# Expert output added to HBM as two scatters of 512 columns, empty places skipped, one gate product moved forward

## The reference, cut to what matters

```python
_, idx = lax.top_k(scores + router_bias, MOE_TOPK)          # 6 of 64 experts for each token
gate = gate / gate.sum(-1, keepdims=True) * ROUTED_SCALE
# routed_experts: token-slots sorted by expert, each expert's rows padded to whole blocks of 128
def run_block(args):
    tok, g, e = args
    return swiglu(x_pad[tok], w_exp_gu[e], w_exp_down[e]) * g[:, None]
return jnp.zeros((T + 1, D), xt.dtype).at[row_tok].add(out.reshape(R, D))[:T]
# moe: routed + swiglu(xt, w_sh_gu, w_sh_down); the layer: layer_norm(ALPHA * x + moe(x))
```

## Time and profile before

| | |
|---|---|
| runs, median (lowest to highest) | 2080.77 us (2078.91 to 2081.96) |
| profiled execution: its time, its span | 2079.63 us, 2077.8 us |
| busy share of PE, DVE, ACT, POOL | 94%, 45%, 27%, 30% |
| DMA in the loop over blocks | share 1.02 of 16 engines, 373 GB/s |
| granted TensorE clock in the loop | 1.00 (2.4 GHz) |

### The profile page before, as it was taken

How to read it: one execution, slowest core, us unless ns; L and a number is a source line. 1 busy time by engine, 2 the same in 40 slices (tenths; PEclk the granted TensorE clock), 3 DMA queues, 4 the chain that set the end, 5 groups by cost and what they waited for, 6 DMA issues and landing times.

```text
span 2077.8 us, 23451 instructions
## 1 busy us (share of the span) xinstructions
PE 1959.6 (94%) x7658; PEld 1084.7 (52%) x7658; DVE 929.9 (45%) x2467; ACT 562.7 (27%) x1147; POOL 618.8 (30%) x792
## 2 busy tenths in 40 slices
PE   8998999999999999999999899999999999999990
PEld 6786645666555665556555463444444444444440
DVE  4374465999765533030344743233332332332324
ACT  2223554562566640030233000111111111111114
POOL 0042000101220001101223254545445555555444
PEclk9999999999999999999999999999999999999995
DMA  6031212110110011134211406999999999999995
GB/s 189 3 38 14 64 41 102 41 47 5 26 26 3 1 31 48 44 132 126 103 61 48 155 31 217 376 369 373 381 373 375 378 373 376 375 373 377 375 364 193
DMA packets 130467, 365.09 MB, mean 176 GB/s; under 512 B 34641, under 2 KB 82514, under 8 KB 112594
## 3 DMA queue, kind: packets, MB, share of 16 engines
q1 hardware_dynamic: 105250, 289.80, 37.2%
q0 software_dynamic: 23328, 72.90, 13.6%
q10 hardware_dynamic: 1808, 1.33, 0.2%
HBM read 310.82 MB, written 53.04 MB: 175 GB/s over the span
## 4 chain that ended last, share of the span: by engine, by line
PE 55%; DMA 19%; DVE 8%; issue 7%; POOL 7%; ACT 2%; POOLq 0%; SPq 0%; DVEq 0%; ACTq 0%
DMA arena<-x_d,tid 17%; PE psum L630 11%; PE psum L774 9%; PE psum L792 6%; PE psum L645 4%; POOL arena L1293 3%; PE psum L845 3%; PE psum L444 3%; POOL acc_d L1287 2%; PE psum L479 2%; PE psum L708 2%; ACT arena L1341 2%; DVE arena L2264 2%; DMA acc_d<-arena,sid 2%; PE psum L491 2%
## 5 line engine op out<-in xcount | busy, mean ns | idle before, releaser
L1341 ACT ACTIVATE arena<-psum 128x512 f32<-128x512 f32 (+8 forms) x643 | 286.0, 486 | 1086.6 <-PE psum L918 429.7
L918 PE MATMUL psum<-arena 128*128 128x512 f32 x1088 | 484.3, 598 | 27.8 <-DVE arena L2264 24.9
L918 PEld LDWEIGHTS psum<-arena 128*128 128x128 f32 x1088 | 201.6, 190 | 267.2 <-issue 265.0
L1293 POOL DMA_INDIRECT arena<-x_d,tid x276 | 264.9, 960 | 85.8 <-issue 71.3
L932 PE MATMUL psum<-arena 128*128 128x512 f32 x544 | 244.7, 593 | 0.5 <-ACT arena L1341 0.5
L630 PE MATMUL psum<-arena 128*128 128x384 f32 (+1 forms) x768 | 239.7, 471 | 0.2 <-DMA arena<-in_w_glu 0.2
L2314 DVE TENSOR_TENSOR arena<-arena,psum 128x256 f32<-128x256 f32 x68 | 28.6, 421 | 457.7 <-ACT arena L1341 457.7
L630 PEld LDWEIGHTS psum<-arena 128*128 128x128 f32 x768 | 144.5, 190 | 94.7 <-issue 10.9
L774 PE MATMUL psum<-arena 128*128 128x384 f32 (+1 forms) x576 | 177.7, 472 | 1.1 <-DVE arena L2075 1.1
L2264 DVE STREAM_TRANSPOSE arena<-arena 128x256 f32<-128x256 f32 x272 | 150.3, 610 | 54.7 <-DMA arena<-x_d,tid 53.7
L932 PEld LDWEIGHTS psum<-arena 128*128 128x128 f32 x544 | 103.5, 190 | 130.0 <-issue 129.4
(11 more groups left out here) (313 smaller groups left out, 2148.1 us busy)
## 6 DMA issues: line engine op xcount, KB each, us to landing
arena<-in_w_exp_gu SPq DMA_DIRECT2D x69, 2048.0 KB, 10.4
arena<-in_w_exp_down SPq DMA_DIRECT2D x68, 1024.0 KB, 10.8
arena<-in_w_in SPq DMA_DIRECT2D x24, 512.0 KB, 4.5
arena<-in_x_prompt SPq DMA_DIRECT2D x10, 512.0 KB, 4.2
arena<-x_d,tid POOLq DMA_INDIRECT x276, 8.8
arena<-in_w_glu SPq DMA_DIRECT2D x16, 256.0 KB, 4.9
arena<-in_w_attn_proj SPq DMA_DIRECT2D x16, 256.0 KB, 4.5
arena<-in_w_out SPq DMA_DIRECT2D x1, 4096.0 KB, 14.4
```

Source lines behind the costliest of these rows:

```text
L918: last = mm(psum[:, 2, :], xgT[u][:, k, :], ewg[u][:, k, :], start=k == 0, stop=k == DK - 1)
L1293: pool.indirect_dma_start(xg[u][:, g, :], None, x1_d.rearrange("t (a f) -> (t a) f", a=4), bass.IndirectOffsetOnAxis(ap=tid[u][:, g:g + 1] ...
L1341: return act.activation(dst, src, fn, **kw)
```

## The change

Three things. Each scatter becomes two of 128 rows of 512 columns. `acc_d` is seen as 2T rows of 512, `sid` holds 2t and 2t + 1 for token t, and the semaphores `y_stored{u}` and `y_half` are split by half, so that a left half waits for the left half of the block before and a right half for the right. The indirect DMAs get a bound (`bounds_check`) of T tokens with `oob_is_err=False`, so that places whose number is T or more, the empty ones, are passed over. And `gate_shared(2)` is called ahead of the first `slots`, not behind the fifth. The rest is renaming: some semaphores are merged so that their number stays within the limit.

```diff
-            def scatter(u, rows_):
-                pool.indirect_dma_start(acc_d, bass.IndirectOffsetOnAxis(ap=sid[u][:, 0:1], axis=0), rows_, None,
-                                        compute_op=ALU.add).then_inc(s(f"y_stored{u}"), 16)
+            def scatter(u, j):
+                pool.indirect_dma_start(half_rows, bass.IndirectOffsetOnAxis(ap=sid[u][:, j:j + 1], axis=0),
+                                        yb[u][:, j * 512:(j + 1) * 512], None,
+                                        bounds_check=2 * T - 1, oob_is_err=False,
+                                        compute_op=ALU.add).then_inc(s(f"y_stored{u}{j}"), 16)
...
-                                            bass.IndirectOffsetOnAxis(ap=tid[u][:, g:g + 1], axis=0)
-                                            ).then_inc(s(f"xg_loaded{u}"), 16)
+                                            bass.IndirectOffsetOnAxis(ap=tid[u][:, g:g + 1], axis=0),
+                                            bounds_check=4 * T - 1, oob_is_err=False).then_inc(s(f"xg_loaded{u}"), 16)
...
-                    pool.wait_ge(s("carried"), n * 2 + 2)
-                    pool.wait_ge(s("sid_ready"), n + 1)
-                    pool.wait_ge(s("y_half"), n * 2 + 2)
-                    pool.wait_ge(s(f"y_stored{1 - u}"), ip * 16 + 16 + 16 * u)
-                    carry_wait()
-                    scatter(u, yb[u])
+                    for j in range(2):
+                        pool.wait_ge(s("carried"), n * 3 + 2 + j)
+                        pool.wait_ge(s("sid_ready"), n + 1)
+                        pool.wait_ge(s(f"y_half{j}"), n + 1)
+                        pool.wait_ge(s(f"y_stored{1 - u}{j}"), ip * 16 + 16 + 16 * u)
+                        carry_wait()
+                        scatter(u, j)
...
             gate_shared(1)
             dve.wait_ge(s("x1_stored"), 16 * NT)
+            gate_shared(2)
             for i in range(NT + 1):
-                if 2 <= i + 1 < NT and i > 0:
+                if 3 <= i + 1 < NT:
                     gate_shared(i + 1)
...
-                dve.wait_ge(s(f"y_stored{u}"), stores)
-                ts(sid[u][:], tab[:, 0, bass.ds(n, 1)], 1.0, None, ALU.mult).then_inc(s("sid_ready"), 1)
+                for j in range(2):
+                    dve.wait_ge(s(f"y_stored{u}{j}"), stores)
+                ts(sid[u][:, 0:1], tab[:, 0, bass.ds(n, 1)], 2.0, None, ALU.mult)
+                ts(sid[u][:, 1:2], tab[:, 0, bass.ds(n, 1)], 2.0, 1.0, ALU.mult, ALU.add).then_inc(s("sid_ready"), 1)
```

More of the change, by code:

```diff
@@ L280, in layer_program @@
         tab4, spread = at(46080, 4, NBP), at(46592, 4, 4, 32)
-        sid = [sb(f"sid{u}", [P, 1], I32) for u in range(2)]
+        sid = [sb(f"sid{u}", [P, 2], I32) for u in range(2)]
         dump = sb("dump", [P, 1])
@@ L1261, in _ @@
                 tt(x, x, ln1[0:r, 1, :], ALU.add).then_inc(s("x1_ready"), 1)
[L1264 to L1265 removed]
+            pool.wait_ge(s("states_and_zeros_stored"), 64 + 16 * 4)
+            pool.wait_ge(s("params_and_dump_ready"), 5)
+            half_rows = acc_d.rearrange("t (j f) -> (t j) f", j=2)
             for u in range(2):
[L1267 to L1270, removed]
+                for j in range(2):
+                    if u == 1:
+                        pool.wait_ge(s(f"y_stored0{j}"), 16)
+                    pool.indirect_dma_start(half_rows, bass.IndirectOffsetOnAxis(ap=sid[u][:, j:j + 1], axis=0),
+                                            ln1[:, u, j * 512:(j + 1) * 512], None, compute_op=ALU.add
+                                            ).then_inc(s(f"y_stored{u}{j}"), 16)
             pool.wait_ge(s("slots_ready"), 1)
@@ L1315, in _ @@
                     gather(1 - u)
-                    pool.wait_ge(s("carried"), n * 2 + 2)
-                    pool.wait_ge(s("sid_ready"), n + 1)
-                    pool.wait_ge(s("y_half"), n * 2 + 2)
-                    pool.wait_ge(s(f"y_stored{1 - u}"), ip * 16 + 16 + 16 * u)
-                    carry_wait()
-                    scatter(u, yb[u])
+                    for j in range(2):
+                        pool.wait_ge(s("carried"), n * 3 + 2 + j)
[4 more added lines that the diff above has]
+                        scatter(u, j)
             for u in range(2):
                 n = last_pair * 2 + u
-                pool.wait_ge(s("carried"), last_pair * 4 + 1 + u)
-                pool.wait_ge(s("sid_ready"), n + 1)
-                pool.wait_ge(s("y_half"), n * 2 + 2)
-                pool.wait_ge(s(f"y_stored{1 - u}"), last_pair * 16 + 16 + 16 * u)
-                carry_wait()
-                scatter(u, yb[u])
+                for j in range(2):
+                    pool.wait_ge(s("carried"), last_pair * 6 + 1 + 2 * u + j)
+                    pool.wait_ge(s("sid_ready"), n + 1)
+                    pool.wait_ge(s(f"y_half{j}"), n + 1)
+                    pool.wait_ge(s(f"y_stored{1 - u}{j}"), last_pair * 16 + 16 + 16 * u)
+                    carry_wait()
+                    scatter(u, j)
             pool.wait_ge(s("ln2_loaded"), 32)
@@ L1694, in _ @@
             dve.tensor_copy(pst[64:80, :].rearrange("q (e n) -> q e n", e=2),
-                            ldt[64:80, :].unsqueeze(2).broadcast_to([GP, 2, NS])).then_inc(s("param_rows"), 1)
+                            ldt[64:80, :].unsqueeze(2).broadcast_to([GP, 2, NS])).then_inc(s("params_and_dump_ready"), 1)
             dve.wait_ge(s("constants"), 10)
             for u in range(2):
-                ts(sid[u][:], dump[:], -1.0, None, ALU.add).then_inc(s("dump_ready"), 1)
+                for j in range(2):
+                    ts(sid[u][:, j:j + 1], dump[:], 2.0, j - 2.0, ALU.mult, ALU.add).then_inc(s("params_and_dump_ready"), 1)
             ar, ai = par[:, 0, :], par[:, 1, :]
```

30 lines of the change are left out of this document (15 added, 15 removed).

## The result

The changed kernel takes 2094.07 us (median of 7 runs, 2085.42 to 2095.67) against 2080.77 us of the kernel before in the same series (7 runs, 2078.91 to 2083.64): ratio 1.0054, 95% interval 1.0036 to 1.0072. The forecast was 2069 us, faster, with a range of 2034 to 2090. The profiled execution took 2092.39 us, its span is 2090.3.

The account below looks back on a forecast made before the run. The prediction took the DMA engines' load to bound the loop, with PE's 10.53 us a block as floor. Terms -1.5 - 12 + 4 + 0 - 2.5 gave -12 us, so 2069 us, with a range of 2034 to 2090.

Parts of the forecast that it names:

- What bounds the kernel: Loop over the blocks: 11.20 us a block against PE's own 10.53, so at most 42 us to win.
- Load: DMA engines in the loop: weights 7.53 and POOL's queue 3.95 us of each engine, 11.48 in a turn of 11.20.
- the chain: Scatters in the loop: landing 10.8 us after issue, the next issued 0.34 us behind it, 11.14 us together.
- Term 1: Gate product ahead of the loop: PE's 9.49 us wait at L827 goes, gain 0.7 to 2.0 us, taken as -1.5.
- Term 2: Empty places passed over, on the DMA engines: between nothing and -42 us, taken near the low end as -12.
- R2: Rival, no relief: pace-setting engine keeps its work or passed-over places cost like filled ones; 2077 to 2081 us, chance 0.17.
- R1: Rival, PE's pace: saving even over engines or shortage shared; -42 in the loop, -4 elsewhere, 2035 us, chance 0.17.
- Term 3: Two half scatters, on the DMA engines: same bytes in twice the rows, at most 20 us, a fifth taken, +4.
- R3: Rival, dear half rows: at 60% of a whole row, 0.54 us a block dearer, 2099 us, slower, chance 0.16.
- Term 4: POOL's issues in the loop: 7.02 us a turn become 9.29 with the second half, below 10.53, so 0 us.
- Term 5: End of the kernel: halves shorten the last chain, whose last link carries almost nothing; bounds -5 to +1, taken -2.5 us.

Follow-up runs that it names:

- e5: Kernel before with half of each down matrix not loaded (output wrong): 2038.12 us, ratio 0.9790.
- e6: Kernel before with whole scatters, empty places passed over in gathers and scatters, and places spread over the partitions: 2045.29 us, ratio 0.9828.
- e4: Kernel before with even and odd blocks added to two tensors, so no scatter waits for the block just before (output incomplete): 2076.76 us, ratio 0.9978.
- e1: Kernel before with only the gate product at its new place: 2080.46 us, ratio 0.9993.
- e10: Kernel before with the gate product moved and empty places passed over, scatters left whole: 2079.62 us, ratio 0.9989.
- e3: Changed kernel with its half scatters alone: no bounds, gate product at its old place: 2103.76 us, ratio 1.0111 to the kernel before.
- e2: Kernel before with only the bounds on gathers and scatters, so empty places are passed over, scatters whole: 2080.07 us, ratio 0.9991.
- e9: Kernel before with whole scatters, empty places passed over, places spread over the partitions and the gate product moved: 2043.76 us, ratio 0.9815.
- e15: Changed kernel with two accumulators, so no loop scatter waits for the block before (output incomplete): 2096.69 us, ratio 1.0073 to the kernel before.
- e7: Changed kernel with the places spread over the partitions: 2072.84 us, runs from 2055.55 to 2083.33, ratio 0.9946 to the kernel before.
- e11: Kernel before with half scatters, nothing passed over, and half of each down matrix not loaded (output wrong): 2042.05 to 2072.26 us, ratio 0.9899.
- e14: Kernel before with half scatters, half of each down matrix not loaded and three gathers a block instead of four: 2034.71 to 2052.32 us, ratio 0.9836.

## Why the prediction was wrong, by its own steps

**What bounds the kernel: right.** Load was taken for the cause and the chain for its echo. e5 and e6 show the one, e4 the other. One of its reasons does not carry: "a share over 1 leaves no room", but e5 has 1.02 and PE never waits. PE's own pace of 10.53 us, the floor of the sum, was reached in e5.

**Term 1, the gate product (-1.5): right in its mechanism, a little high.** The wait at L827 went, and PE waits for the one-hot rows. Between the first `shared_down` and block 4 PE gains 0.7 us on the kernel before, in e1, in e10 and in the changed kernel alike: the lower bound. In the changed kernel's profile more than that is lost before it starts. The timeline of PE at this place:

```profile
1143.52 9.04 PE L845 MATMUL psum<-arena 128*128 128x512 f32 x16
...
1164.59 0.39 PE L827 MATMUL psum<-ident,arena 128*128 128x128 f32 x2
...
1186.29 6.65 PE L891 MATMUL psum<-arena 128*128 128x234 f32 x18 [3.58 <-DVE arena L2316]
...
1199.86 3.60 PE L836 MATMUL psum<-arena 128*128 128x512 f32 x8
```

The `shared_down` behind the one-hot rows starts at 1199.86, 2.1 us later than before. PE came late from ahead of it: the `shared_up` of 16 instructions at 1143.52 took 9.04 us, before 7.13, and the first `shared_down` started 2.8 us late. The table by stage says why (busy us, granted clock, DMA share, GB/s), first of the changed kernel:

```profile
1140.00:1145.00 5.00, 4.42 (x22) 3.55 (x23) 1.80 (x9) 1.29 (x2) 3.06 (x2) 0.56 0.81 105
...
1160.00:1172.00 12.00, 11.53 (x32) 5.47 (x31) 10.73 (x33) 1.16 (x4) 0.00 (x0) 1.00 0.01 0
```

and of the kernel before:

```profile
1140.00:1145.00 5.00, 4.04 (x26) 2.72 (x27) 3.05 (x11) 2.01 (x4) 0.31 (x2) 1.00 0.69 107
...
1160.00:1172.00 12.00, 2.50 (x8) 1.16 (x7) 11.24 (x26) 0.00 (x0) 0.00 (x0) 0.68 0.01 0
```

The granted clock was 0.56 (near 1.2 of 2.4 GHz) where it had been 1.00, ahead of the place that the change touches; before, it dipped to 0.68 behind PE's idle time at L827, and with that idle time gone it stays at 1.00. What made the earlier dip no run tells. It isn't the moved product: e3, which has it at its old place, shows 0.66 in the same five us and 8.83 us for that `shared_up`, and e2 has 1.00.

**Term 2, skipped places (-12): the step that failed first.** "I take a value near the low end" was the right direction, but the low end itself came: e2's period is before's. The mechanism behind it was read rightly (the empties are always the high partitions, so some engine keeps its rows), and e6 bears it out. What failed is the amount that the fullest engine was to be spared, 6.2 us from empty fourth gathers and 5.9 us from the second blocks. Neither shows in the 63 blocks. A passed-over place still sends a packet, which the sum had at zero; whether that or an engine that is spared even less eats the 12 us, the runs don't say. This was rival R2 for this term (0.17). Of R1's 46 us, e9 got 37 once the placement was changed.

**Term 3, the halves (+4): the step that turned the sign.** The bound from above was 20 us, from the price of a gather's row, 0.039 us. e3 measured 22 us in all, and 14.5 stand between e10 and the changed kernel. A period longer by 0.29 us for 8 more rows of each engine is 0.036 us a row, if all of it is the rows. The choice of a fifth of the bound, since "a 1 KB row is mostly bytes", was the mis-sized step: an added row costs nearly what a whole small row costs. R3 named the mechanism. It set its turning point at 0.32 us a block by counting 12 us of term 2 as saved; with nothing saved there, 4 us of gain elsewhere are used up at 0.06 us a block, and the 0.21 us measured decide it. With the -12 left out the sum is 2069 + 12 = 2081, no change; with term 3 at 14.5 as well it is 2091.5, near the 2094 measured. R3's row price came out smaller than the 60% it was given: (2.70 + 0.29) / 16 = 0.19 us for a half against 0.34 for a whole, 55%, an estimate that rests on the queue's packet time for the 2.70.

**Term 4, POOL (0): right.** 9.29 us a turn were worked out, 9.65 stand in the timeline above (a bounded gather takes 1.04 us on average instead of 0.96, and a half scatter is issued no faster than a whole, 1.61 us). e15 shows POOL waiting for data. The 10.3 to 10.4 us that three of the expectations name held waits for the two halves of the output. What the term missed is the chain behind the second half, which costs nothing at the changed kernel's pace (e15) and shows where the loop could run faster.

**Term 5, the end (-2.5): right in size, but hardly by the halves.** The timeline of the end:

```profile
2044.74 1.56 POOL L1292 DMA_INDIRECT acc_d<-arena,sid  x1 [0.51 <-POOL carry L1306]
2045.48 0.75 DVE L2336 TENSOR_SCALAR arena<-psum,gcol 128x512 f32<-128x512 f32 x1 [1.09 <-PE psum L932]
...
2048.88 1.56 POOL L1292 DMA_INDIRECT acc_d<-arena,sid  x1 [0.50 <-issue]
2051.70 4.30 SPq L954 DMA_DIRECT2D arena<-acc_d  x9
```

From the last `gate_and_up` to SP's loads it is 2051.70 - 2030.40 = 21.3 us, before 25.1: -3.8, inside the bounds. Passing over the empties does it by itself: -4.0 in e2 and -3.6 in e10, with whole scatters, and -0.7 in e3, with halves and nothing passed over. What holds of the term's reasons is the last link that carries no token; it landed 2.8 us after its issue. So the halves brought next to nothing here either.

**The sum as measured**, between the two profiled spans: block 4 starts 2.1 us later (2.8 from the dip of the clock, less 0.7 of term 1), the loop takes 13.2 us more, the way to SP's loads 3.8 less, and what is behind them 1.0 more (38.6 us to the end of the span, before 37.6): +12.5 us. The range (up to 2090) missed the median by 4 us: it took in only the cheap third of R3, and gave R3 0.16.

**Open.** Which engine is the fullest, and the price of one packet: no view names an engine for a packet, and the cost of the halves in the full loop was found by taking the other causes away, not by measuring it alone. The queue's packet time doesn't confirm it in the changed kernel: 0.300 x 11.41 = 3.42 us of each engine in a block, with whole scatters (e2) 0.312 x 11.21 = 3.50. Why e7, e11 and e14 vary from run to run with the same program is told by place (the chain), not by cause; only one run of each was profiled.

## What to carry to other kernels

A saving in bytes counts only where the fullest DMA engine gets it: in an indirect transfer, ask which partitions are spared, and spread them before anything else (here 35 us for one table of places). Don't split an accumulating scatter on full DMA engines; the rows are paid, not only the bytes (here 14 to 22 us). And when two limits lie close together, here load at 11.2 to 11.4, PE at 10.53 us and the chain of landings somewhere between, what an edit costs depends on which of the others is relieved: test it at each.

## What the runs showed that I had not expected

- A place beyond the bound is not free: queue 0 has as many packets with a quarter of the places passed over (14875) as without (14946), and a gather with the bound takes POOL 1.04 us to issue for 0.96.
- Taking the chain away at full load made nothing faster (e15 2096.7 against 2094.1), although POOL had waited for it 111 us.
- The DMA share is 1.02 in e5, with PE never waiting, and 1.00 in the changed kernel, with PE waiting in 58 places: it can't tell full engines from fitting ones. Nor is the time of a queue's packets a price: unchanged gathers and scatters took 3.95 us of each engine in a block before and 4.30 in e5.
- Nearly the whole gain at the end, 4 us, came from passing over the empty block, not from the halves.
